# Expert values of the prompt gathered by token instead of by slot

## The reference, cut to what matters

```python
v1, i1 = lax.top_k(s1, 16); v2, i2 = lax.top_k(s2, 16)      # per head, of 128 keys each
sc, ci = lax.top_k(cand, 16)                                 # of the sums v1 + v2
expert = ia * 128 + ib
gate = softmax(sc)
a = einsum('chkd,cd->chk', u_tab[expert], xc)                # rows of peer_u, 1024 floats each
wgt = gate * gelu(a)
y = einsum('chk,chkd->cd', wgt, v_tab[expert])               # rows of peer_v, 1024 floats each
```

## Time and profile before

| what | value |
|---|---|
| three runs, median (lowest to highest) | 1873.16 us (1870.47 to 1877.69) |
| the profiled execution, its own time | 1872.7 us |
| its span, first to last instruction | 1870.9 us |
| mean granted TensorE clock | 0.951 |
| busy: PE, DVE, ACT, POOL | 1479.4, 1055.4, 373.1, 1212.5 us |
| moved by DMA | 618.34 MB, mean 331 GB/s |
| of it by POOL's queue (U and V gathers nearly all) | 571.18 MB |
| first U gather starts | 323.91 us |

### The profile page before, as it was taken

The page is one execution under the profiler, slowest core; times in us unless marked ns, Lnnn a source line. Parts: engine busy times, 40 slices in busy tenths (PEclk is TensorE's granted clock), DMA queues, the critical chain, the costliest instruction groups (busy, mean ns, idle before and its releaser), DMA issues.

```text
span 1870.9 us, 14659 instructions
## 1 busy us (share of the span) xinstructions
PE 1479.4 (79%) x4385; PEld 628.6 (34%) x4385; DVE 1055.4 (56%) x2681; ACT 373.1 (20%) x891; POOL 1212.5 (65%) x1291
## 2 busy tenths in 40 slices
PE   8974887879599677768986677799777777777789
PEld 4553563423144222223432222244222222222233
DVE  4945414866948954445698444448954445444430
ACT  2233231022122111111221111112221111111111
POOL 0007500587776777777677777777777777777763
PEclk9987689899799999999998999999899999999999
DMA  8026071789998999999989999999999999999996
GB/s 325 30 70 165 27 304 50 261 309 338 355 345 328 345 365 409 382 372 411 407 325 337 369 408 408 408 410 347 352 360 410 409 410 410 409 410 409 409 394 229
DMA packets 171054, 618.34 MB, mean 331 GB/s; under 512 B 19728, under 2 KB 25184, under 8 KB 169984
## 3 DMA queue, kind: packets, MB, share of 16 engines
q0 software_dynamic: 156928, 571.18, 79.7%
q1 hardware_dynamic: 14048, 46.22, 7.3%
HBM read 610.52 MB, written 5.19 MB: 329 GB/s over the span
## 4 chain that ended last, share of the span: by engine, by line
POOL 25%; PE 19%; DVE 16%; DMA 14%; issue 9%; ACT 1%; DVEq 0%
PE sb_peer_acc L1546 15%; POOL sb_peer_U L1186 14%; DMA sb_kept_V<-peer_v,sb_kept_expert 13%; POOL sb_kept_V L1195 12%; DVE sb_peer_U L1352 4%; PE sb_peer_pq L1471 3%; DVE sb_peer_hot L1287 1%; DVE sb_peer_f L1290 1%; DVE sb_peer_idx L1239 1%; DVE sb_peer_idx L1231 1%; DVE sb_peer_left L1232 1%; DMA sb_peer_U<-peer_u,sb_kept_expert 1%; DVE sb_peer_val L1236 1%; DVE sb_peer_hot L1289 1%; DMA sb_peer_U<-peer_u,sb_peer_es 1%
## 5 line engine op out<-in xcount | busy, mean ns | idle before, releaser
L1546 PE MATMUL sb_peer_acc<-sb_kept_V,sb_peer_dg 128*128 128x512 f32 (+1 forms) x2176 | 1049.5, 617 | 308.1 <-DMA sb_kept_V<-peer_v,sb_kept_expert 212.6
L1352 DVE CUSTOM_DVE_ANT_0 sb_peer_U<-sb_peer_U,sb_rows_xn 128x1024 f32<-128x1024 f32 x512 | 619.8, 1224 | 545.6 <-DMA sb_peer_U<-peer_u,sb_kept_expert 538.7
L1546 PEld LDWEIGHTS sb_peer_acc<-sb_kept_V,sb_peer_dg 128*128 128x128 f32 (+1 forms) x2176 | 379.1, 188 | 954.4 <-issue 500.1
L1186 POOL DMA_INDIRECT sb_peer_U<-peer_u,sb_kept_expert x512 | 531.1, 1037 | 184.4 <-issue 151.1
L1195 POOL DMA_INDIRECT sb_kept_V<-peer_v,sb_kept_expert x512 | 538.8, 1052 | 170.1 <-issue 105.4
L1428 ACT ACTIVATE sb_peer_dg<-sb_kept_ident,sb_peer_wt 128x128 f32<-128x128 f32 (+1 forms) x544 | 210.8, 395 | 1064.7 <-PE sb_peer_acc L1546 832.6
L1186 POOL DMA_INDIRECT sb_peer_U<-peer_u,sb_peer_es x32 | 39.8, 1243 | 127.0 <-DVE sb_peer_es L1291 105.5
L1471 PE MATMUL sb_peer_pq<-sb_rows_wq,sb_peer_xnT 128*128 128x512 f32 x256 | 115.5, 605 | 1.1 <-ACT sb_peer_xnT L1380 1.1
L626 POOL MEMSET sb_rows_wq<- 16x4096 f32 x1 | 3.5, 3506 | 117.1 <-POOLq L161 117.1
L463 PE MATMUL sb_proj_pz<-sb_proj_w_in,sb_proj_xT 128*128 128x512 f32 (+1 forms) x192 | 72.4, 539 | 7.9 <-DVE sb_proj_xT L292 7.9
L1471 PEld LDWEIGHTS sb_peer_pq<-sb_rows_wq,sb_peer_xnT 128*128 128x128 f32 x256 | 49.5, 194 | 64.7 <-issue 63.1
(11 more groups left out here) (259 smaller groups left out, 989.7 us busy)
## 6 DMA issues: line engine op xcount, KB each, us to landing
sb_peer_U<-peer_u,sb_kept_expert POOLq DMA_INDIRECT x512, 6.6
sb_kept_V<-peer_v,sb_kept_expert POOLq DMA_INDIRECT x512, 6.6
sb_proj_w_in<-w_in SPq DMA_DIRECT2D x8, 640.0 KB, 10.8
sb_kept_V<-w_out SPq DMA_DIRECT2D x1, 4096.0 KB, 15.4
sb_proj_xT<-xT SPq DMA_DIRECT2D x8, 272.0 KB, 9.7
sb_proj_x<-x_tok SPq DMA_DIRECT2D x4, 512.0 KB, 12.4
sb_proj_w_mem<-w_mem SPq DMA_DIRECT2D x1, 2048.0 KB, 19.7
sb_blend_MT<-sb_rows_wq SPq DMA_DIRECT2D x8, 256.0 KB, 10.0
```

What stands on the lines that cost most here:

```text
L1186: pool.indirect_dma_start(U[:, n % RU, :], None, d["peer_u"], bass.IndirectOffsetOnAxis(ap=rows(n), axis=0)).then_inc(s_u[n % RU], 16)
L1352: dve.tensor_tensor_reduce(U[:, n % RU, :], U[:, n % RU, :], x, 1.0, 0.0, ALU.mult, ALU.add, a[:, g % 2, n % GRP:n % GRP + 1]).then_inc(s_ ...
L1546: mm = pe.matmul(acc[:r, c, :], dg[:, n % RD, 0:r], V[:, n % RV, c * 512:(c + 1) * 512], start=(s == 0), stop=(s == count[k] - 1))
```

## The change

The samples are handled as before. For prompt tiles the V gather takes the rows of one token: partition p receives the row of slot p, so a step m of a prompt tile is now one token. For that, DVE writes the expert numbers as floats too (`ef`), PE transposes them, and DVE copies them to `eT`, where a column is a token's list. The weights of a tile are kept whole (`wt`), transposed by PE and copied by ACT to `wT`. ACT puts four tokens' weight columns at a time into the middle of zeroed 63-wide strips (`spot`); PE takes 32 columns of a strip such that the weight column stands at the token's place, and sums into one quarter of `acc`. Steps take the quarters in turn (j = s % 4, place r = s // 4). Each token's matmuls release its V buffer by themselves.

Since a token needs all its 128 weights, V now runs 130 steps behind U (`LAGV`). From step 66 to step 161 POOL gathers U alone, and after the last U, 130 V gathers remain. The schedule of the parts is also new: queries of tile 2 at 62 + 24b, of tiles 3 and 4 at 10 + 24b into the tile before them, with routes 14 steps behind. The routes fall at steps 16, 48, 56, 64 (tile 1), 76, 100, 124, 148 (tile 2), 184, 208, 232, 256 (tile 3) and 312, 336, 360, 384 (tile 4). `turn_experts` stands 18 steps behind the last query of a tile, `turn_weights` 2 steps into the next tile. ACT's norms of tiles 2 to 4 move into its loop, and gelu runs one group later in ACT's loop, weights at step 18 + 16g.

```diff
-        LAG = 34
-        WEIGH = LAG - 1
-        ROWS_OUT, QTURN, QUERY_OUT, SCORE, EXPS, ROUTE, GATES = 3, 4, 7, 8, 22, 50, 62
-        query = {(1, b): 8 * (b - 1) for b in range(1, 4)}
-        query.update({(k, b): first[k - 1] + 6 + 8 * b for k in range(2, NT) for b in range(4)})
+        LAG, LAGV = 34, SLOTS + 2
+        WEIGH = GRP + 2
+        ROWS_OUT, QTURN, QUERY_OUT, SCORE, ROUTE, EXPS, GATES = 3, 4, 6, 7, 14, 16, 24
+        EXPERTS_TURN, EXPERTS_OUT = 18, 20
+        query = {(1, b): 34 + 8 * (b - 1) for b in range(1, 4)}
+        query.update({(2, b): 62 + 24 * b for b in range(4)})
+        query.update({(k, b): first[k - 1] + 10 + 24 * b for k in range(3, NT) for b in range(4)})
...
             def _(pool):
+                    if n - LAGV >= first[1]:
+                        m = n - LAGV
+                        k, s = steps[m]
+                        if s == 0:
+                            pool.wait_ge(s_ee, k)
+                        pool.wait_ge(s_mm, m - RV + 1)
+                        t = s % 4 * NSMP + s // 4
+                        pool.indirect_dma_start(V[:, m % RV, :], None, d["peer_v"],
+                                                bass.IndirectOffsetOnAxis(ap=eT[:, k - 1, t:t + 1], axis=0)).then_inc(s_v[m % RV], 16)
...
+                def experts_by_token(k):
+                    dve.wait_ge(s_et, k)
+                    dve.tensor_copy(eT[:, k - 1, :], psc[:, 3, 0:P]).then_inc(s_ee, 1)
...
-                    dst, src = (dg[:, n % RD, :], K.ident[:, :]) if k else (dg[:, n % RD, 0:NSMP], ident4[:, :])
-                    act.activation(dst, src, ACT.Copy, scale=wt[:, g % 2, n % GRP:n % GRP + 1]).then_inc(s_dg, 1)
+                        act.activation(dg[:, m % RD, :], ident4[:, :], ACT.Copy, scale=wt[:, 0, m:m + 1]).then_inc(s_dg, 1)
+                    for k in range(1, NT):
+                        if n == first[k + 1] + 2:
+                            act.wait_ge(s_wx, k)
...
+                            act.activation(wT[:, k % 2, :], psc[:, 0, 0:P], ACT.Copy).then_inc(s_we, 1)
...
+                        act.activation(spot[:, v % RW, :, NSMP - 1], wT[:, k % 2, :].rearrange("p (j r) -> p j r", r=NSMP)[:, :, s // 4],
+                                       ACT.Copy).then_inc(s_spot, 1)
...
+                def turn_experts(k):
+                    pe.wait_ge(s_id, part(k, 3) + 1)
+                    pe.transpose(psc[:, 3, 0:P], ef[:, k % 2, :], K.ident[:, :]).then_inc(s_et, 1)
+
+                def turn_weights(k):
+                    pe.wait_ge(s_wt, first[k + 1] // GRP)
...
+                    pe.transpose(psc[:, 0, 0:P], wt[:, k % 2, :], K.ident[:, :]).then_inc(s_wx, 1)
...
+                def add_token(m):
+                    k, s = steps[m]
+                    v, r, j = (m - first[1]) // 4, s // 4, s % 4
+                    if s == 0:
+                        pe.wait_ge(s_y, k)
+                    if j == 0:
+                        pe.wait_ge(s_spot, v + 1)
+                    pe.wait_ge(s_v[m % RV], 16 * (m // RV + 1))
+                    for c in range(2):
+                        mm = pe.matmul(acc[j * NSMP:(j + 1) * NSMP, c, :], spot[:, v % RW, j, NSMP - 1 - r:2 * NSMP - 1 - r],
+                                       V[:, m % RV, c * 512:(c + 1) * 512], start=(r == 0), stop=(r == NSMP - 1))
+                    mm.then_inc(s_mm, 1)
```

More of the change, by code:

```diff
@@ L1173, in _ @@
             def _(pool):
[L1175 to L1179, removed]
+                for n in range(NSTEP):
                     if n < NS:
@@ L1185, in _ @@
                             pool.wait_ge(s_dot, n - RU + 1)
+                        row = K.expert[:, order[k], s:s + 1] if k else es[:, s:s + 1]
                         pool.indirect_dma_start(U[:, n % RU, :], None, d["peer_u"],
-                                                bass.IndirectOffsetOnAxis(ap=rows(n), axis=0)).then_inc(s_u[n % RU], 16)
-                    m = n - LAG
-                    if m >= 0:
+                                                bass.IndirectOffsetOnAxis(ap=row, axis=0)).then_inc(s_u[n % RU], 16)
+                    if 0 <= n - LAG < first[1]:
+                        m = n - LAG
                         if m == 0:
@@ L1329, in _ @@
                 dve.wait_ge(s_xs, 64)
[L1330 to L1336, removed]
+                for n in range(NSTEP):
+                    if n >= WEIGH and (n - WEIGH) % GRP == 0 and (n - WEIGH) // GRP < NG:
                         weights((n - WEIGH) // GRP)
@@ L1343, in _ @@
                         gates(*kb)
-                    if k and s == RESULT:
-                        result(k - 1)
+                    for k, b in due(n, EXPERTS_OUT):
+                        if b == 3:
+                            experts_by_token(k)
+                    if n == first[1] + LAG + 2:
+                        result(0)
+                    for k in range(1, NT - 1):
+                        if n == first[k + 1] + LAGV + 2:
+                            result(k)
                     if n == ROUTE0:
@@ L1349, in _ @@
                         route(*kb)
[L1350 to L1355, removed]
+                    if n < NS:
+                        k, s = steps[n]
+                        g = n // GRP
+                        if n % GRP == 0 and g >= 2:
+                            dve.wait_ge(s_ga, g - 1)
+                        dve.wait_ge(s_u[n % RU], 16 * (n // RU + 1))
+                        x = K.xn[:, order[k], :] if k else xs[:, :]
+                        dve.tensor_tensor_reduce(U[:, n % RU, :], U[:, n % RU, :], x, 1.0, 0.0, ALU.mult, ALU.add,
+                                                 a[:, g % 2, n % GRP:n % GRP + 1]).then_inc(s_dot, 1)
                 result(NT - 1)
@@ L1403, in _ @@
                 exps(1, 0)
[L1404 to L1412, removed]
+                act.wait_ge(s_zero, 1)
+                for n in range(NSTEP + 4):
+                    if n in RESIDUAL:
+                        norm(2 + RESIDUAL.index(n))
+                    for k, b in due(n, TURN_OUT):
+                        if k >= 2 and b == 0:
+                            turned_out(k)
                     for kb in due(n, ROWS_OUT):
@@ L1418, in _ @@
                         exps(*kb)
[L1419 removed]
+                    if n % GRP == 0 and 1 <= n // GRP <= NG:
+                        g = n // GRP - 1
                         act.wait_ge(s_dot, GRP * (g + 1))
@@ L1540, in _ @@
                         scores(*kb)
[L1541 to L1548, removed]
+                    for k, b in due(n, EXPERTS_TURN):
+                        if b == 3:
+                            turn_experts(k)
+                    for k in range(1, NT):
+                        if n == first[k + 1] + 2:
+                            turn_weights(k)
+                    if 0 <= n - LAG < first[1]:
+                        add_sample_rows(n - LAG)
+                    m = n - LAGV - 3
+                    if first[1] <= m < NS:
+                        add_token(m)
 class Kept:
```

77 lines of the change are left out of this document (59 added, 18 removed).

## The result

The changed kernel takes 1933.21 us (median of 4 runs, 1926.9 to 1933.88) against 1873.9 of before: ratio 1.0308, interval 1.0279 to 1.0338, slower. The forecast had 1896. The profiled execution took 1933.74 us, its span is 1931.9.

A forecast was written before the change was run, and what follows sets the result against it. The expert part was taken as transfer bound at 410 GB/s, starved around routes, and PE bound after the last dot; 1872.7 - 80.6 (B) - 3.5 (C) + 107.7 (D) = 1896 us, range 1850 to 1940.

The forecast's parts named there:

- A: Stretch up to step 66, 507.7 us before; claimed change 0 (range -3 to +3).
- D: Stretch from the last dot to the last matmul: 169.6 us instead of 61.9, +107.7, with V 130 steps behind.
- The rival in which the groups do not overlap: In D, PE holds the next token back until the fourth record is through: 1.72 us a token, 1953 us; chance 0.09.
- the rival of slow rows by token: V gathers by token take 1.46 us, lengthening C and D: 1988 us; chance 0.04.
- C: Steps 162 to 543: 975 us floor plus 8 routes, 1027 us, -3.5 (-55 to +31).
- B: Steps 66 to 161, POOL gathering U alone: 186 us instead of 266.6, -80.6 (-96 to -69).
- Thirteen steps at 1.28: In B's 24-step cycle, the steps after the eleventh dot take 1.28 us each, giving 45.1.
- The walk: Sum through one 24-step cycle of B with a 14.4 us route: 46.4 us; four cycles make 186.
- The upper bound of 198: Longest B: gathers alone at the pace of the first sixteen, 96 x 1.46 + 58 us.
- I take 6.5: In C, each of 8 routes, 24 steps apart, costs 6.5 us: 975 + 52 = 1027.
- The three rows: Profiled costs of routes with free running behind them, 6.7, 10.8 and 6.2 us, used for the route price in C.
- Routes vanish in C: Rival: 24 steps refill both rings, a route costs about 1 us, C takes 983, total 1852 us; chance 0.17.

The follow-up runs named there:

- bunched run: Changed kernel with its routes of tiles 2 to 4 eight steps apart instead of 24, all else kept: 1894.38 us (1.0092).
- pieces and x in PSUM: Changed kernel with x in PSUM and each route of tiles 2 to 4 cut into best values, sums and numbers, five steps apart: 1827.61 us (0.9734).

## Why the prediction was off

- The direction and the account were right: the change moves V's transfers behind the last dot. A lies 5 us below its value (2 below its lower bound); no run tells why, and by luck it hides part of the miss. D is right to 1.3 us, and the run with one column group shows that its reason is right too. The rival in which the groups do not overlap falls with it. So does the rival of slow rows by token: 409 GB/s in C's undisturbed slices and in D's, where V alone is gathered.
- B (186 forecast, 204.9 measured) failed at "Thirteen steps at 1.28". The walk let the slowing end after four gathers. But U alone, at a step of 1.28 us, is so close to the dot's 1.15 that gathers and dots keep meeting: the three full cycles from dot 76 to dot 148 took 50.3, 50.2 and 51.6 us, not 46.4, 13 us in all. The other 6 us stand in the ten steps before and the fourteen behind, where the one gather of 7.79 us falls. With x in PSUM a cycle is 43.6 (dot 100 to dot 124), less than the walk. The upper bound of 198 failed with it: it took 1.46 us for the slowest pace, and behind a route it was 1.64 over 22 gathers. A small slip is in the walk as well: 22.8 + 6.04 is 28.8, not 28.5, which is 1.4 us in four cycles.
- C (1027 forecast, 1049.0 measured) failed at "I take 6.5". The three rows gave 6.7, 10.8 and 6.2; I took the low pair and argued that 24 steps cut the recovery short. The runs show the reverse: bunched routes cost 6.6 and 6.9, those that stand alone 9.2 here and 11.1 in the kernel before. A reading that fits the trace of the bunched run: while the next route stops the dots, POOL catches up (under the route of 798.8 to 813.5 us there its gathers take 0.94 to 0.95 us). The row with the longest free stretch, 10.8, came nearest to what spread routes cost.
- Behind both stands one missing cause. The text saw the slow gathers and counted them, but gave as the reason only that "DVE works off filled buffers", and so carried a number from one place to another where it doesn't hold. What counts is whether a gather starts while a dot with two SBUF operands runs. The edit that removes the cause, x in PSUM, takes 41 us from C and 27 from B.
- "Routes vanish in C" was wrong for this kernel and is nearly what happens once the cause is gone (0.7 us a route with pieces and x in PSUM).

Open: how much of the spread routes' price in the changed kernel is wait and how much slow gathers. Where POOL's time in C went can be counted: with spread routes it waited 28.7 us for dots and its gathers took 66.5 us beyond 0.945 each, with bunched ones 14.8 and 60.5. So 14 of C's 21 us stand as wait there; in the kernel before it is the other way round, 10 us of wait and 32 of slow gathers between the two placements. This is a count of POOL's time and not a cause: with x in PSUM the slow gathers go, POOL waits more (69.0 us), and C is still 41 us shorter. Bunched routes with x in PSUM were not run in the changed kernel.

## What to carry to other kernels

Before spreading work out or cutting it up, ask what slows the neighbour engine while the backlog is worked off; a price measured in one arrangement is the price of that arrangement, and the longest undisturbed stretch in the trace is the one to read. Where POOL issues gathers, an operand that DVE reads again and again belongs in PSUM: here one copy per tile, with no longer instruction, brought nearly every gather behind step 66 to 0.94 us and made the kernel before 1.85% faster, 4.6% with the long DVE work spread and in pieces.

## What the runs showed of the hardware

- A POOL gather of 128 rows of 4 KB takes 0.94 us and the next starts 0.30 later, however busy DVE is, as long as DVE reads one operand of the dot from SBUF. A gather that starts while a dot with two SBUF operands runs takes 0.94 us plus the rest of that dot less 0.13 (130 of 130 in before), so up to 1.99; in three runs one gather was held through six dots, 7.79 us.
- The other way round, a dot that starts inside a running gather is not held (1.22 us). Where a gather starts less than 0.03 us behind a dot, the gather takes 0.94 us and the dot 0.04 to 0.06 longer than 1.22 (four in after).
- The dot of 128x1024 takes 1218 ns with x in PSUM and 1223 with x in SBUF.
- A token's four records follow each other every 1.285 us, at the pace of the transfer, when its neighbours use other column groups, and every 1.726 when they use the same.
